# A hybrid encoder layer on one Trainium2 core: attention products one step later, the exponential ahead of the high part on ScalarE, and four smaller moves

## The chip, the cores and the metric

The kernel runs on one core of one Trainium2 chip, written in Bass with every engine's instruction stream and semaphores laid out by hand. The metric is device time in microseconds (us), the median of several executions; lower is better. Engines are named as in the profile: PE is TensorE (PEld its weight loads), DVE is VectorE, ACT is ScalarE, POOL is GpSimd, SP is SyncE, which issues most DMAs.

## The reference, cut to what matters

One encoder layer over 512 tokens of 1024 features: a long-convolution mixer and a grouped-query attention side by side, then attention over 256 memory rows, then a mixture of 16 experts. The change touches the attention and the two stages behind it:

```python
def attend_block(qblk):
    s = jnp.einsum('bkgqd,bksd->bkgqs', qblk, kt).astype(jnp.float32) * scale
    p = jax.nn.softmax(s, axis=-1).astype(vt.dtype)
    return jnp.einsum('bkgqs,bksd->bkgqd', p, vt)
...
y = jnp.concatenate([group_rms_norm(y_hy, out_norm_hyena[i], HYENA_GROUPS),
                     group_rms_norm(y_at, out_norm_attn[i], N_Q_HEADS)], axis=-1)
x = x + y @ w_out[i]
x = x + memory_cross_attn(rms_norm(x, norm_xattn[i]), rms_norm(mem, norm_mem[i]), ...)
x = x + hier_moe(rms_norm(x, norm_moe[i]), ...)
```

There are 8 query heads of 64 features over 2 key/value heads, and in the memory attention 4 heads of 128, whose keys are normalised per head by a root mean square and a gain.

## The kernel before, in words

Products that need more than one pass of precision are made from a high part (the value rounded to fp32r, by ScalarE) and a low part (value less high part, by VectorE), as three products: high by high, high by low, low by high. Weights come from HBM in pieces of 512 KB through a ring of three buffers: ScalarE makes `w_hi` of a piece (`weight_hi`, L744), VectorE `w_lo` (`weight_lo`, L1173), TensorE multiplies (`chunk_jobs`, L1987). Pieces 26 to 29 are the first half of the output projection (`wo0`), 30 to 33 the second (`wo1`), 34 to 37 the memory queries (`wq`).

**The attention loop** has 32 steps, one for 128 queries of one head. Step s, engine by engine:

- TensorE (`for s in range(-2, NSEQ)`): `score(s + 4)`, two products into a PSUM bank; `pt(s + 2)`, four transposes of the exponentials; at listed steps a transpose of further queries or keys (`QT_STEPS`, `KT_STEPS`), of the last head's output (`out_T`, `OT_STEPS`), the sums of squares of the convolution's output (`HN_STEPS`) or the transposes of its inverse norms (`hyena_inverse_T`, `HR_STEPS`); and at odd steps `pv(s // 2)`, the eight products with the values for steps s-1 and s.
- ScalarE: `gqa_pt_hi(s)`, the high part of the transposed exponentials (L911), then `gqa_exp(s + 2)` (L903), then at listed steps copies out of PSUM (`out_copy` L918, `out_rows` L924, `qT_evac` L880, `kT_evac` L876), squares (L884), a weight piece's high part, and once the square root of the convolution's sums (`hyena_root`, L889), which needs another activation table.
- VectorE: `gqa_max(s + 3)` (a reduction L1499 and a tiny product L1500), then `gqa_lo(s)`, the low part (L1506), then at listed steps a weight piece's low part, `out_sums` (L1512) and `hyena_norm` (L1477, L1484, L1485).
- GpSimd: `out_square` (L604), for the two memory row blocks `mk_normed` (L596, L597), and one copy that widens the 32 inverse norms of the convolution to `inv_wide` (L612).

A transposed pair of steps sits in one of two buffers, so `gqa_pt_hi(s)` waits until `pv(s // 2 - 2)` is done. Scores and transposes turn through six PSUM banks. `psum_jobs` is the one list by which every engine counts banks, so each table of steps is used there too.

**Behind the loop** TensorE transposes the normalised attention output (`yT_job`, four of them), finishes `wo0` (piece 29 needs all four), runs `wo1`, transposes the memory keys (`mkT`, which wait for `mk_normed`), then x, and multiplies `wq`. ScalarE makes the four high parts `yT_hi` (L749) and after them the pieces from 29 on. Then comes the memory attention: eight steps of score, exponential, normalisation by VectorE and transposes (L1932), and the products with the memory values (`mo`, L1925). The router and the experts follow; their instructions are not touched.

`constant_products(job, n)` (L1963) multiplies the identity by itself n times into a bank that will be overwritten; it computes nothing that is used.

Of the kernel before, what the change touches and what calls it, by code (L numbers as in the profile page):

```python
# [57 lines left out]

HR_STEPS = [17, 20, 24, 28]
GATED_STEP = 1  # L60
HN_STEPS = [8, 12]
MK_STEP = 9
QT_STEPS = [1, 5, 9, 11, 13, 15]
KT_STEPS = [3, 7]
EARLY = NQ - 2
EARLY_STEP = TT * EARLY + 5
OT_STEPS = [TT * h + 6 for h in range(NQ - 1)]
FILL = [3, 3, 2, 2] + [1] * 6


def psum_jobs():
# [21 lines left out]
    for s in range(-2, n):  # L93
        if s >= 0 and s % TT == 1:
            jobs += [("O", s // TT)]
        if s + 2 + AHEAD < n:
            jobs += [("S", s + 2 + AHEAD)]
        if s + 2 < n:
            jobs += [("PT", s + 2)]
        if s in OT_STEPS:  # L100
            jobs += [("OT", OT_STEPS.index(s))]
        if s in KT_STEPS:
            jobs += [("kT", 2 + KT_STEPS.index(s))]
        if s in QT_STEPS:
            jobs += [("qT", 2 + QT_STEPS.index(s))]
        if s in HN_STEPS:
            jobs += [("hn", HN_STEPS.index(s))]
        if s in HR_STEPS:
            jobs += [("hr", HR_STEPS.index(s))]
# [21 lines left out]
def build(nc, a, out, xn_dram, y_dram):  # L131
    with ExitStack() as ctx:
# [235 lines left out]
        s_pair = sem("ident_pair_ready")  # L368
        s_minv = sem("mk_inverse_ready")
        s_store = sem("xn_stored")  # L370
# [207 lines left out]
        def _(pool):  # L578
# [12 lines left out]
            pool.tensor_tensor(ident_pair[:], ident[:, 0:HD], ident[:, HD:P], ALU.add).then_inc(s_pair, 1)  # L591
            def mk_normed(j):

                pool.wait_ge(s_minv, 1)
                x3 = mk[:, j, :].rearrange("p (h d) -> p h d", d=MHD)
                link(pool.tensor_tensor(x3, x3, small[:, 40 + MH * j:44 + MH * j].unsqueeze(2).to_broadcast([P, MH, MHD]), ALU.mult))  # L596
                pool.tensor_tensor(x3, x3, row("gmk").unsqueeze(1).to_broadcast([P, MH, MHD]), ALU.mult).then_inc(s_mkn, 1)  # L597

            def out_square(h):

                wait_freed(pool, ("OT", h))
                if h >= 2:
                    pool.wait_ge(s_oss, h - 1)
                pool.tensor_tensor(o_sq[:, h % 2], out_head(h), out_head(h), ALU.mult).then_inc(s_osq, 1)  # L604

            out_square(0)
            mk_normed(0)
            out_square(1)
            mk_normed(1)
            out_square(2)  # L610
            pool.wait_ge(s_hrec, 1)
            pool.tensor_copy(inv_wide[:].rearrange("p t c w d -> p (t c w) d"),  # L612
                             small[:, 280:312].unsqueeze(2).to_broadcast([P, 8 * TT, HD])).then_inc(s_hwide, 1)

            for h in range(3, NQ):
                out_square(h)
# [68 lines left out]
        def _(act):  # L685
# [200 lines left out]
            def hyena_root():  # L886
                for n in range(len(HN_STEPS)):
                    wait_freed(act, ("hn", n))
                act.activation(small[:, 280:312], small[:, 280:312], ACT.Sqrt, bias=eps, scale=1.0 / HD).then_inc(s_hroot, 1)  # L889

            kT_evac(0)
            kT_evac(1)
# [41 lines left out]
            for s in range(NSEQ):  # L934
                gqa_pt_hi(s)
                if s + AHEAD < NSEQ:
                    gqa_exp(s + AHEAD)
                if s % TT == 0 and s > 0:
                    out_copy(s // TT - 1)
# [8 lines left out]
                if s == HN_STEPS[-1] + 1:  # L948
                    hyena_root()
                if s in (8, 10, 19):  # L950
                    weight_hi(26 + (8, 10, 19).index(s), 1)
                if s == EARLY_STEP:
                    act.activation(small[:, 398:399], eps, ACT.Sqrt)
                    out_root(0, EARLY, 4)
            out_copy(NQ - 1)
            out_rows(NQ - 1)
            out_root(EARLY, NQ, 5)
            for k in range(CT):
                split_hi(("yT", k), yT_hi[:, CT + k, :], col("attn_norm", k))
            weight_hi(29, 6)  # L960

# [181 lines left out]
        def _(dve):  # L1143
# [392 lines left out]
            for s in range(AHEAD + 1):  # L1536
                gqa_max(s)
            dve.wait_ge(s_hrms, 1)
            dve.reciprocal(small[:, 40:48], small[:, 40:48]).then_inc(s_minv, 1)
            dve.wait_ge(s_vhi, 1)  # L1540
# [35 lines left out]
            dve.wait_ge(ld["x2"], 16 * TT)  # L1576
            for k in range(CT):
                split_lo(("yT", k), yT_lo[:, CT + k, :], yT_hi[:, CT + k, :], col("attn_norm", k))
            weight_lo(29, 3)
            residual("wout", 0)  # L1580
            weight_lo(32, 4)
            residual("wout", 1)
# [335 lines left out]
        def _(pe):  # L1918
# [211 lines left out]
            def hyena_inverse_T(c):  # L2130

                if c == 0:
                    pe.wait_ge(s_hwide, 1)
                transposes(("hr", c), [inv_wide[:, t, c].rearrange("p w d -> p (w d)") for t in range(TT)])
# [65 lines left out]
            for s in range(-2, NSEQ):  # L2200
# [14 lines left out]
                for m in range(2 * (s - NSEQ) + 6, 2 * (s - NSEQ) + 8):  # L2215
                    if m >= 0:
                        output_tile(wo0 + m // TT, m % TT)
                if s >= 0 and s % 2 == 1:
                    pv(s // 2)
            output_tile(wo0 + 1, 2)  # L2220
# [38 lines left out]
            for s in range(MSEQ):  # L2259
                if s + MAHEAD < MSEQ:  # L2260
                    mem_score(s + MAHEAD)
                pe.wait_ge(s_mnorm, s + 1)
                transposes(("MPT", s), [pr[:, s % NPR, k * P:(k + 1) * P] for k in range(4)])
            for s in range(MSEQ):
                wait_freed(pe, ("MPT", s))
# [287 lines left out]
```

## Time and profile before

| what | us |
|---|---|
| median of 3 runs | 800.45 (798.2 to 801.01) |
| the profiled execution | 800.26 |
| its span (first to last instruction) | 798.4 |
| PE busy in the span | 748.8 |
| DVE busy | 605.4 |
| ACT busy | 460.1 |
| POOL busy | 86.2 |

The span is what the trace covers; the execution's own time is 1.86 us longer. Times in rows are us from the span's start. A matmul's row lasts from its start to the modelled end, so matmuls in a row overlap; the pitch is read from start to start. The same holds for ScalarE and VectorE, whose next instruction may start some 0.1 us before the last one's end. The attention loop lies at 258 to 346 us, the output projection to 387, the memory attention to 444, the router to 500, the experts to the end.

### The profile page before, as it was taken

To read this page: it belongs to the slowest core of one execution; us is meant where nothing else is said; L and a number is where in the kernel's file an instruction comes from. 1 tells how busy PE (TensorE), PEld (TensorE's weight loads), DVE (VectorE), ACT (ScalarE), POOL (GpSimd) and SP (SyncE) were. 2 spreads that over 40 slices of the span, in tenths; PEclk is the share of its full clock that TensorE was granted. 3 is DMA by queue.
4 is the path that set the end of the run, shared out by engine and by line. 5 is a ranking of instruction groups with operands and counts; after the bars stand their busy time and mean duration, and the time that the engine had idled before them with its cause. 6 is when DMAs were issued, how large, how long until landed. Compare 5 with 4: busy or idle time off the path is not lost.

```text
span 798.4 us, 10807 instructions
## 1 busy us (share of the span) xinstructions
PE 748.8 (94%) x3644; PEld 605.1 (76%) x3644; DVE 605.4 (76%) x926; ACT 460.1 (58%) x685; POOL 86.2 (11%) x99
## 2 busy tenths in 40 slices
PE   5899999999999888979897999999999999999994
PEld 3665858788898876768784787888888888888883
DVE  5767483996799879833547468899989989999882
ACT  5942333221243887531558332788788888887772
POOL 0000000000000022000000001123223233222111
PEclk9999999999999999999998997999999999999997
DMA  8730303020130200022130665999999999999841
GB/s 291 293 106 1 89 17 106 28 79 1 53 88 20 106 1 2 1 79 80 53 106 27 218 263 219 385 380 371 376 371 382 382 385 376 369 368 381 308 163 20
DMA packets 28542, 146.53 MB, mean 184 GB/s; under 512 B 4791, under 2 KB 6711, under 8 KB 21976
## 3 DMA queue, kind: packets, MB, share of 16 engines
q1 hardware_dynamic: 23320, 135.53, 45.5%
q0 software_dynamic: 5184, 10.50, 5.0%
q8 instruction: 23, 0.38, 0.2%
q14 instruction: 15, 0.12, 0.0%
HBM read 141.81 MB, written 12.58 MB: 193 GB/s over the span
## 4 chain that ended last, share of the span: by engine, by line
PE 70%; DVE 16%; ACT 6%; DMA 4%; issue 3%; SPq 0%; POOL 0%; DVEq 0%; ACTq 0%; POOLq 0%
PE bank L1987 17%; PE bank L2372 10%; PE bank L2374 10%; PE bank L2373 10%; PE bank L1925 10%; PE bank L1932 2%; DMA slot<-in_w_down 2%; PE bank L2367 2%; PE bank L1999 1%; DVE w_lo L1173 1%; DVE small L1499 1%; ACT w_hi L744 1%; ACT pr L1003 1%; PE bank L2286 1%; PE bank L2284 1%
## 5 line engine op out<-in xcount | busy, mean ns | idle before, releaser
L1844 DVE TENSOR_TENSOR e_lo<-slot,e_hi 128x1024 fp32r<-128x1024 f32 x192 | 221.5, 1219 | 9.8 <-ACT e_hi L1053 9.7
L1053 ACT ACTIVATE e_hi<-slot 128x1024 fp32r<-128x1024 f32 x192 | 188.2, 1060 | 8.5 <-DMA slot<-in_w_down 5.8
L1173 DVE TENSOR_TENSOR w_lo<-w_raw,w_hi 128x1024 fp32r<-128x1024 f32 x41 | 50.1, 1239 | 71.8 <-ACT w_hi L744 71.7
L744 ACT ACTIVATE w_hi<-w_raw 128x1024 fp32r<-128x1024 f32 x41 | 42.6, 1057 | 100.4 <-DMA w_raw<-in_w_in 63.4
L2372 PE MATMUL bank<-e_hi,hgT_hi 128*128 128x512 f32 x240 | 95.0, 396 | 0.3 <-DVE hgT_lo L1856 0.3
L2374 PE MATMUL bank<-e_hi,hgT_lo 128*128 128x512 f32 x240 | 93.6, 390 | 0.0
L2373 PE MATMUL bank<-e_lo,hgT_hi 128*128 128x512 f32 x240 | 93.4, 389 | 0.0
L2372 PEld LDWEIGHTS bank<-e_hi,hgT_hi 128*128 128x128 f32 x240 | 45.2, 189 | 9.5 <-DVE hgT_lo L1856 0.7
L2374 PEld LDWEIGHTS bank<-e_hi,hgT_lo 128*128 128x128 f32 x240 | 45.0, 188 | 9.6
L2373 PEld LDWEIGHTS bank<-e_lo,hgT_hi 128*128 128x128 f32 x240 | 45.1, 188 | 8.9
L2372 PE MATMUL bank<-e_hi,gaT_hi 128*128 128x512 f32 x120 | 48.1, 400 | 0.0
L2374 PE MATMUL bank<-e_hi,gaT_lo 128*128 128x512 f32 x120 | 46.9, 391 | 0.0
L2373 PE MATMUL bank<-e_lo,gaT_hi 128*128 128x512 f32 x120 | 46.8, 390 | 0.0
L1987 PE MATMUL bank<-hT_hi,w_hi 128*128 128x512 f32 x96 | 37.9, 395 | 0.0
L1987 PE MATMUL bank<-hT_lo,w_hi 128*128 128x512 f32 x96 | 37.4, 389 | 0.0
L1987 PE MATMUL bank<-hT_hi,w_lo 128*128 128x512 f32 x96 | 37.4, 389 | 0.0
L1987 PE MATMUL bank<-w_hi,hT_hi 128*128 128x512 f32 (+1 forms) x96 | 34.0, 354 | 0.8 <-DVE hT_lo L1179 0.8
L1987 PE MATMUL bank<-w_hi,hT_lo 128*128 128x512 f32 (+1 forms) x96 | 34.0, 354 | 0.0
L1987 PE MATMUL bank<-w_lo,hT_hi 128*128 128x512 f32 (+1 forms) x96 | 34.0, 354 | 0.0
L1932 PE MATMUL bank<-ident,pr 128*128 128x128 f32 x160 | 24.8, 278 | 9.6 <-ACT pr L903 5.3
L653 POOL DMA_INDIRECT out_dram<-eo,meta_i x16 | 25.5, 1595 | 74.5 <-ACT eo L1088 44.3
L1071 ACT ACTIVATE hgT_hi<-bank 128x512 fp32r<-128x512 f32 x28 | 15.2, 595 | 30.5 <-PE bank L2367 30.5
(395 smaller groups left out, 1674.5 us busy)
## 6 DMA issues: line engine op xcount, KB each, us to landing
slot<-in_w_down SPq DMA_DIRECT2D x16, 2048.0 KB, 17.1
slot<-in_w_gate SPq DMA_DIRECT2D x16, 2048.0 KB, 14.9
slot<-in_w_up SPq DMA_DIRECT2D x16, 2048.0 KB, 15.6
w_raw<-in_w_in SPq DMA_DIRECT2D x18, 512.0 KB, 3.6
w_raw<-in_w_out SPq DMA_DIRECT2D x8, 512.0 KB, 3.7
w_raw<-in_w_k_mem SPq DMA_DIRECT2D x4, 512.0 KB, 6.2
x_in<-in_x SPq DMA_DIRECT2D x4, 512.0 KB, 9.3
w_raw<-in_w_v_mem SPq DMA_DIRECT2D x4, 512.0 KB, 6.1
```

The source lines that it names most:

```text
L653: pool.indirect_dma_start(out[0], bass.IndirectOffsetOnAxis(ap=meta_i[:, q, 0:1], axis=0), eo[q][:], None, bounds_check=T - 1, oob_is_err= ...
L744: act.activation(w_hi[ring(m)][:], w_raw[ring(m)][:], ACT.Copy).then_inc(s_wh, 1)
L1053: act.activation(e_hi[buffer(b, j)][:], slot[slot_][:, 1024 * part:1024 * (part + 1)], ACT.Copy).then_inc(s_ehi, 1)
L1173: dve.tensor_tensor(w_lo[slot_][:], w_raw[slot_][:], w_hi[slot_][:].bitcast(F32), ALU.subtract)\
L1844: dve.tensor_tensor(e_lo[slot_][:, at_], slot[slot_][:, at_], e_hi[buffer(b, j)][:].bitcast(F32), ALU.subtract)\
L1925: ins = pe.matmul(dst, l, r, start=(n == 0), stop=(n == len(pairs) - 1))
L1932: ins = pe.transpose(bank(job)[:, n * width:(n + 1) * width], s, ident[:])
L1987: ins = pe.matmul(bank(job)[:, 0:width], left, right, start=(k == 0 and m == 0), stop=(final and m == 2))
L2367: ins = pe.transpose(banks[half][:, k * P:(k + 1) * P], hg[q][:, c:D:KT], ident[:])
L2372: pe.matmul(dst, act_hi, w_hi_, start=first, stop=False)
L2373: pe.matmul(dst, act_hi, w_lo_, start=False, stop=False)
L2374: return pe.matmul(dst, act_lo, w_hi_, start=False, stop=last)
```

## The change

1. `pv` of a pair runs one step later on TensorE: at even steps, with the last pair after the loop. The tables of steps shift to suit.
2. ScalarE runs `gqa_exp(s + 2)` before `gqa_pt_hi(s)`; `out_copy` comes one step later.
3. Weight: the high and low part of piece 29 are made before the fourth `yT` split, not after it.
4. Inverse: `inv_wide` is written by ScalarE in four parts, one for each use, not by GpSimd in one copy.
5. Keys: the memory keys are normalised by VectorE in the output projection, not by GpSimd in the attention loop.
6. Constants: constant products are added before each transpose job of the memory attention (6, then 1 each) and before its value products (5).

```diff
-HR_STEPS = [17, 20, 24, 28]
+HR_STEPS = [17, 21, 25, 29]
-HN_STEPS = [8, 12]
+HN_STEPS = [9, 13]
-QT_STEPS = [1, 5, 9, 11, 13, 15]
-KT_STEPS = [3, 7]
+QT_STEPS = [1, 5, 8, 10, 12, 14]
+KT_STEPS = [3, 6]
-EARLY_STEP = TT * EARLY + 5
-OT_STEPS = [TT * h + 6 for h in range(NQ - 1)]
+EARLY_STEP = TT * EARLY + 6
+OT_STEPS = [TT * h + 7 for h in range(NQ - 1)]
...
-            out_square(0)
-            mk_normed(0)
-            out_square(1)
-            mk_normed(1)
-            out_square(2)
-            pool.wait_ge(s_hrec, 1)
-            pool.tensor_copy(inv_wide[:].rearrange("p t c w d -> p (t c w) d"),
-                             small[:, 280:312].unsqueeze(2).to_broadcast([P, 8 * TT, HD])).then_inc(s_hwide, 1)
-            for h in range(3, NQ):
+            for h in range(NQ):
                 out_square(h)
...
+            def inverse_wide(c):
+                act.wait_ge(s_hrec, 1)
+                act.activation(inv_wide[:, :, c], small[:, 280:312].rearrange("p (t c w) -> p t c w", t=TT, c=CT)[:, :, c, :]
+                               .unsqueeze(3).to_broadcast([P, TT, 2, HD]), ACT.Copy).then_inc(s_hwide, 1)
...
             for s in range(NSEQ):
-                gqa_pt_hi(s)
                 if s + AHEAD < NSEQ:
                     gqa_exp(s + AHEAD)
-                if s % TT == 0 and s > 0:
+                gqa_pt_hi(s)
+                if s % TT == 1 and s > 1:
                     out_copy(s // TT - 1)
...
+                if s + 1 in HR_STEPS:
+                    inverse_wide(HR_STEPS.index(s + 1))
...
             for k in range(CT):
+                if k == CT - 1:
+                    weight_hi(29, 1)
                 split_hi(("yT", k), yT_hi[:, CT + k, :], col("attn_norm", k))
-            weight_hi(29, 6)
+            weight_hi(30, 5)
...
             for k in range(CT):
+                if k == CT - 1:
+                    weight_lo(29, 1)
                 split_lo(("yT", k), yT_lo[:, CT + k, :], yT_hi[:, CT + k, :], col("attn_norm", k))
-            weight_lo(29, 3)
+            weight_lo(30, 2)
             residual("wout", 0)
-            weight_lo(32, 4)
+            dve.wait_ge(s_hrms, 1)
+            link(dve.reciprocal(small[:, 40:48], small[:, 40:48]))
+            weight_lo(32, 1)
+            mk_normed(0)
+            weight_lo(33, 1)
+            mk_normed(1)
+            weight_lo(34, 2)
             residual("wout", 1)
...
-                if c == 0:
-                    pe.wait_ge(s_hwide, 1)
+                pe.wait_ge(s_hwide, c + 1)
...
-                if s >= 0 and s % 2 == 1:
-                    pv(s // 2)
+                if s > 0 and s % 2 == 0:
+                    pv(s // 2 - 1)
+            pv(2 * NQ - 1)
...
                 if s + MAHEAD < MSEQ:
                     mem_score(s + MAHEAD)
+                constant_products(("MPT", s), 6 if s == 0 else 1)
                 pe.wait_ge(s_mnorm, s + 1)
                 transposes(("MPT", s), [pr[:, s % NPR, k * P:(k + 1) * P] for k in range(4)])
+            constant_products(("mo", 0), 5)
```

The first place is ScalarE at steps 2 to 5 of the attention loop. The name `pr` is the exponential, `pT_hi` the high part, `oT` the copy of a head's output. Before:

```order
L911 ACTIVATE pT_hi<-bank 128x4x128
L903 ACTIVATE pr,small<-bank,small 128x512
L880 ACTIVATE qT<-bank 128x512
L884 ACTIVATE y_sq<-u 128x512
L911 ACTIVATE pT_hi<-bank 128x4x128
L903 ACTIVATE pr,small<-bank,small 128x512
L884 ACTIVATE y_sq<-u 128x512
L911 ACTIVATE pT_hi<-bank 128x4x128
L903 ACTIVATE pr,small<-bank,small 128x512
L918 ACTIVATE oT<-bank 128x512
```

And now:

```order
L891 ACTIVATE pr,small<-bank,small 128x512
L899 ACTIVATE pT_hi<-bank 128x4x128
L867 ACTIVATE y_sq<-u 128x512
L891 ACTIVATE pr,small<-bank,small 128x512
L899 ACTIVATE pT_hi<-bank 128x4x128
L859 ACTIVATE kT<-bank 128x512
L867 ACTIVATE y_sq<-u 128x512
L891 ACTIVATE pr,small<-bank,small 128x512
L899 ACTIVATE pT_hi<-bank 128x4x128
L906 ACTIVATE oT<-bank 128x512
```

Within a step the exponential now stands ahead of the high part, and the copy `oT` stands behind the next step's pair of them.

The second place is ScalarE behind the loop, at the four high parts of `yT`. Before:

```order
L930 ACTIVATE small<-small 128x4x2
L749 ACTIVATE yT_hi<-bank,cols 128x512 x4
L744 ACTIVATE w_hi_59<-w_raw_51 128x1024
L744 ACTIVATE w_hi_57<-w_raw_49 128x1024
L744 ACTIVATE w_hi_58<-w_raw_50 128x1024
```

And now:

```order
L918 ACTIVATE small<-small 128x4x2
L732 ACTIVATE yT_hi<-bank,cols 128x512 x3
L727 ACTIVATE w_hi_59<-w_raw_51 128x1024
L732 ACTIVATE yT_hi<-bank,cols 128x512
L727 ACTIVATE w_hi_57<-w_raw_49 128x1024
L727 ACTIVATE w_hi_58<-w_raw_50 128x1024
```

The first piece (29, in buffer 51) moved ahead of the fourth high part; VectorE's `w_lo` moved in the same way.

The third place is TensorE in the memory attention, from the first scores on. Before:

```order
L1932 MATMUL bank<-ident,mq 128x128 x16
L2253 MATMUL bank<-mkT,mqT 128x256 x8
L1932 MATMUL bank<-ident,pr 128x128 x4
L2253 MATMUL bank<-mkT,mqT 128x256 x2
L1932 MATMUL bank<-ident,pr 128x128 x4
```

And now:

```order
L1938 MATMUL bank<-ident,mq 128x128 x16
L2259 MATMUL bank<-mkT,mqT 128x256 x8
L1969 MATMUL bank<-ident 128x128 x6
L1938 MATMUL bank<-ident,pr 128x128 x4
L2259 MATMUL bank<-mkT,mqT 128x256 x2
L1969 MATMUL bank<-ident 128x128
L1938 MATMUL bank<-ident,pr 128x128 x4
```

Constant products (L1969) now stand in front of every transpose job; nothing else moved there.

## Rows read from the trace of the kernel before

**Rows 1.** Stretch, length, busy us (count) of PE, PEld, DVE, ACT, POOL; PEclk, DMA, GB/s

```profile
259.38:330.75 71.37, 60.73 (x449) 53.28 (x448) 60.95 (x119) 57.81 (x125) 10.44 (x11) 1.00 0.08 30
354.87:357.85 2.98, 0.00 (x1) 0.00 (x1) 2.03 (x3) 2.58 (x3) 0.00 (x0) 1.00 0.60 176
357.85:361.80 3.95, 3.95 (x10) 3.12 (x11) 2.90 (x3) 1.06 (x1) 0.00 (x0) 0.57 0.01 4
434.72:440.30 5.58, 5.58 (x7) 2.48 (x8) 4.19 (x4) 2.98 (x4) 0.00 (x0) 0.50 0.00 0
430.00:434.70 4.70, 1.98 (x13) 1.27 (x13) 2.35 (x10) 4.13 (x11) 0.00 (x0) 0.87 0.00 0
```

**Rows 2.** Waits, 259 to 331 us: total us, times, longest

```profile
ACT oT L918 <- PE bank L1925: 5.5, 7, 1.1
PE bank L1932 <- ACT pr L903: 5.3, 5, 2.5
PE bank L1925 <- DVE pT_lo L1506: 3.5, 4, 1.7
```

**Rows 3.** Timeline of PE, one wait early in the loop (start, length, [idle before])

```profile
273.36 0.49 PE L1963 MATMUL bank<-ident 128*128 128x128 f32 x2 [1.34 <-ACT pr L903]
```

**Rows 4.** Timeline of ACT and PE around the square root

```profile
293.54 1.28 ACT L889 ACT_TABLE_LOAD   x1 [1.40 <-DVE small L1493]
297.96 0.63 PE L1932 MATMUL bank<-ident,pr 128*128 128x128 f32 x4 [2.46 <-ACT pr L903]
```

**Rows 5.** GpSimd's copy, VectorE's tiny product beside it, and that product's usual length

```profile
300.49 1.90 POOL L612 COPY inv_wide<-small 128x2048 f32<-128x2048 f32 x1
300.72 1.68 DVE L1500 TENSOR_TENSOR small<-small 128x1 f32<-128x1 f32 x1
L1500 DVE TENSOR_TENSOR small<-small x32: 159/160/1680, 259.2 to 328.2; 128x1 f32<-128x1 f32 x32
```

**Rows 6.** Timeline of DVE: one step and the work on the convolution's output

```profile
304.31 0.41 DVE L1512 TENSOR_REDUCE small<-o_sq 128x4 f32<-128x256 f32 x1
304.63 0.68 DVE L1499 TENSOR_REDUCE small<-bank 128x1 f32<-128x512 f32 x1
305.43 0.69 DVE L1506 TENSOR_TENSOR pT_lo<-bank,pT_hi 128x512 fp32r<-128x512 f32 x1
306.03 0.74 DVE L1477 SCALAR_TENSOR_TENSOR u<-u,cols,bank 128x512 f32<-128x512 f32 x1
...
307.88 0.69 DVE L1499 TENSOR_REDUCE small<-bank 128x1 f32<-128x512 f32 x1
```

**Rows 7.** Timeline of ACT: one step; and the squares of 128x512 from SBUF

```profile
302.79 0.60 ACT L911 ACTIVATE pT_hi<-bank 128x512 fp32r<-128x512 f32 x1
303.27 0.79 ACT L903 ACTIVATE pr<-bank,small 128x512 f32<-128x512 f32 x1
...
304.03 0.62 ACT L911 ACTIVATE pT_hi<-bank 128x512 fp32r<-128x512 f32 x1
...
L884 ACT ACTIVATE y_sq<-u x4: 618/634/646, 266.2 to 273.2; 128x512 f32<-128x512 f32 x4
```

**Rows 8.** The load of piece 29, and such loads' time to landing

```profile
338.87 0.38 SPq L494 DMA_DIRECT2D w_raw<-in_w_out  x1
...
w_raw<-in_w_out SPq DMA_DIRECT2D x8, 512.0 KB, 3.7
```

**Rows 9.** Timeline at piece 29: ACT, DVE, PE

```profile
354.90 0.69 ACT L749 ACTIVATE yT_hi<-bank,cols 128x512 fp32r<-128x512 f32 x1 [6.21 <-PE bank L1932]
355.62 0.75 DVE L1179 SCALAR_TENSOR_TENSOR yT_lo<-bank,cols,yT_hi 128x512 fp32r<-128x512 f32 x1 [5.72 <-ACT yT_hi L749]
357.85 0.50 PE L1987 MATMUL bank<-w_hi,yT_hi 128*128 128x512 f32 x1 [2.98 <-DVE w_lo L1173]
```

**Rows 10.** Timeline of PE: two products of 128x512 in `wo0`, before that

```profile
353.58 0.39 PE L1987 MATMUL bank<-w_hi,yT_hi 128*128 128x512 f32 x1
353.81 0.39 PE L1987 MATMUL bank<-w_lo,yT_hi 128*128 128x512 f32 x1
```

More of the change, by code:

```diff
@@ L93, in psum_jobs @@
     for s in range(-2, n):
-        if s >= 0 and s % TT == 1:
+        if s >= 0 and s % TT == 2:
             jobs += [("O", s // TT)]
@@ L368, in build @@
         s_pair = sem("ident_pair_ready")
-        s_minv = sem("mk_inverse_ready")
         s_store = sem("xn_stored")
@@ L591, in _ @@
             pool.tensor_tensor(ident_pair[:], ident[:, 0:HD], ident[:, HD:P], ALU.add).then_inc(s_pair, 1)
[L592 to L597, printed above, removed]
             def out_square(h):
@@ L954, in _ @@
                     out_root(0, EARLY, 4)
+            out_rows(NQ - 2)
             out_copy(NQ - 1)
@@ L1537, in _ @@
                 gqa_max(s)
-            dve.wait_ge(s_hrms, 1)
-            dve.reciprocal(small[:, 40:48], small[:, 40:48]).then_inc(s_minv, 1)
             dve.wait_ge(s_vhi, 1)
@@ L1577, in _, with mk_normed @@
             for k in range(CT):
+                if k == CT - 1:
+                    weight_lo(29, 1)
                 split_lo(("yT", k), yT_lo[:, CT + k, :], yT_hi[:, CT + k, :], col("attn_norm", k))
-            weight_lo(29, 3)
+            weight_lo(30, 2)
             residual("wout", 0)
-            weight_lo(32, 4)
+            def mk_normed(j):
+                x3 = mk[:, j, :].rearrange("p (h d) -> p h d", d=MHD)
+                link(dve.tensor_tensor(x3, x3, small[:, 40 + MH * j:44 + MH * j].unsqueeze(2).to_broadcast([P, MH, MHD]), ALU.mult))
+                dve.tensor_tensor(x3, x3, row("gmk").unsqueeze(1).to_broadcast([P, MH, MHD]), ALU.mult).then_inc(s_mkn, 1)
+            dve.wait_ge(s_hrms, 1)
[5 more added lines that the diff above has]
+            weight_lo(34, 2)
             residual("wout", 1)
```

## The prediction

> **What bounds the kernel now.** I read the stretches first (busy time and granted clock), then the waits of the attention loop, then the timelines of ACT, DVE and PE at the places that the change touches, and last the load of piece 29. TensorE is busy 748.8 of the 798.4 us, so time is to be had only where it waits or runs at the lower clock. [Rows 1] show four such places: the loop up to its last exponential, 71.37 us of which TensorE works 60.73, so 10.6 us is the most that the loop can give; 2.98 us without a product ahead of piece 29; the 3.95 us behind that at a granted clock of 0.57, which is near the lower of TensorE's two levels (1.2 against 2.4 GHz); and 5.58 us at 0.50 in the memory attention, with TensorE busy throughout. What is saved there should last to the end: from the memory attention on, the work hangs on TensorE's progress, and the experts keep it busy.
>
> In the loop no engine is full: DVE works 60.95 and ACT 57.81 of 71.37. The waits in [rows 2] are a ring: TensorE's transposes wait for exponentials (5.3 us), its value products for low parts (3.5 us), ScalarE's copy of a head's output for TensorE (5.5 us in 7).
>
> **The change, part by part, against the profiled execution's own 800.26** (the median of the runs is 800.45, so nothing has to be shifted).
>
> *Values one step later.* The copy `oT` no longer stands in ScalarE's queue waiting for products just issued: they are a step old. At the first place where this reaches TensorE the wait is 1.34 us [rows 3]; I take 1.3 off. The copy waited 5.5 us in all, but most of that lay beside TensorE's own work, so no more is taken. Nothing of TensorE's work is added; the last pair of products moves behind the loop, where only the last head's output waits for it.
>
> *The square root.* ScalarE's queue holds a table load of 1.28 us behind a wait of 1.40, and TensorE then waits 2.46 [rows 4]. With one exponential more issued ahead of the root, and VectorE's sums no longer behind a weight piece, I take the wait to be 1.8: 0.65 off. Ends: 0 (the table load stays as it is, and decides) and 1.4.
>
> *Inverse and keys off GpSimd.* Beside GpSimd's copy of 1.90 us VectorE's tiny product took 1.68 us, where its usual time is 0.16 [rows 5]. So VectorE's chain gets back 1.5 us. The Trainium skill says in "SBUF — State Buffer", section "Who interferes with whom", that VectorE and GpSimd share a pair of ports as an exclusive lock, which blocks a VectorE operation with two SBUF inputs beside a GpSimd one that reads SBUF; the trace agrees, with the 1.68 against 0.16. VectorE's 1.5 us is TensorE's too where the ring binds, and I take all of it; the lower end is 0 (TensorE waits for ScalarE's root there anyway). In return VectorE gets four multiplications and one reciprocal in the output projection. Each is no longer than its 0.74 us of 128x512 [rows 6], together 3.2 us; VectorE waits for TensorE in that stage (5.72 us at one place, below), which covers them, and without that cover they would cost up to 3.2. I take 0. ScalarE gets four parts, each of 128x512 elements as `y_sq` is: about 0.63 us each [rows 7], 0.52 where the next starts early, 2.1 us in all.
>
> *Exponential ahead of the high part.* This has a price. VectorE's step is 0.80 us for the maximum and its product, 0.60 for the low part; a sum of squares 0.32, a step of the convolution's norm 1.85 (306.03 to 307.88) [rows 6]. ScalarE's is 0.76 for the exponential, 0.48 for the high part, whose result is there after 0.60 [rows 7]. Count from VectorE's maximum for step 22, at 0: it is there at 0.80, exp(22) ends at 1.58, high part 20 is there at 2.18, and VectorE comes to low part 20 at 2.20: no stall. Now ScalarE does a copy and an inverse part (0.8), exp(23) ends at 3.6, high part 21 is there at 4.19 against 3.61 wanted: 0.6 lost. The copy `oT` (0.49) in the next step gives 5.91 against 5.6: 0.3 lost. The norm's 1.85 then lets ScalarE catch up. So 0.9 per group of four steps where inverse parts are made, three groups, 2.7 us. Against it stand TensorE's waits for low parts, 3.5 us in 4 [rows 2], which exponentials issued sooner should shorten; I set 1.5 against it and book 1.2 as cost. Ends: −2.3 (all 3.5 go, and the ring costs only 1.2) and +2.7 (none goes). The Trainium skill says in "TensorE: Matmul & The Clock Gate", section "Architectural detail: the array is 16× 32×32, not 1× 128×128", that ScalarE's and VectorE's queues keep strict order. That speaks against this edit: a ready high part stays behind an exponential whose maximum is late. Read by itself, it would turn the 1.2 into the full 2.7.
>
> *The last inverse* stands between exponentials of steps 30 and 31 now; the transposes of the fourth block come later by its 0.5. I book 0.5.
>
> **Loop:** −1.3 −0.65 −1.5 +1.2 +0.5 = −1.8 us (rounded).
>
> *Weight.* Piece 29 is issued at 338.87 and such a load lands after 3.7 us [rows 8], so at 342.6. ScalarE is idle 6.21 us before the fourth `yT_hi` at 354.90, VectorE 5.72 before `yT_lo` at 355.62 [rows 9]; w_hi and w_lo (at most 0.95 and 1.3 us, by what is left of the second stretch of [rows 1] beside those rows) fit in. TensorE then waits for `yT_lo` alone, ready at 355.62 + 0.75 = 356.37, and starts at 356.45 instead of 357.85: 1.4 off. Three of the 24 products of that piece don't need `yT_lo` of the fourth and run in the wait, at a pitch of 0.23 [rows 10]: 0.7 off. The ends are 1.0 and 2.8.
>
> *Clock behind piece 29.* The stretch at 0.57 holds 10 products in 3.95 us [rows 1]; at 0.23 they take 2.3: 1.6 off, if the clock stays up. Before it TensorE had 2.98 us without a product; now it would have about 1.2. In the loop it waits 2.46 [rows 4] while the granted clock of the loop stays at 1.00 [rows 1]. So I expect it to stay. Ends: 0 and 1.6.
>
> *Constants.* 18 constant products of 128x128, two of which take 0.49 us [rows 3]: 4.4 us at most. Before the low stretch TensorE works 1.98 of 4.70 us while ScalarE works 4.13 [rows 1]; the 6 and the first ones fill 2.7 of idle there, and the last 5 stand where the value products wait for ScalarE's high parts. So they cost about 0, and at most 4.4 − 2.7 = 1.7. If they hold the clock, 5.58 us at 0.50 become 2.79: 2.8 off. If they don't: 0.
>
> **Sum:** 1.8 + 2.1 + 1.6 + 2.8 = 8.3; 800.26 − 8.3 = 792.0 us.
>
> **The rivals.** About 0.5% (4 us) is what a measurement of this kernel can tell from no change.
>
> 1. *The ring is looser than worked out.* ScalarE has 13 us free in the loop, and all waits for low parts go: the loop gives 1.8 + 1.2 + 3.5 = 6.5, the time is 787.3. Against it: the same engines carry 2 us more.
>
> 2. *The clock doesn't do what the edits want.* The constants are few, and single ones between steps may not hold it: 5.5 gained, 794.8. If only the stretch behind piece 29 stays low, 6.7 gained, 793.6. Both low: 1.8 + 2.1 = 3.9, 796.4. For it: the clock fell after a stretch in which TensorE worked 1.98 of 4.70, and gaps between the single constants remain. This is also the case in which that part of the change doesn't do what it says.
>
> 3. *The order on ScalarE binds in every head.* The 0.9 us are lost in seven groups of four steps instead of three, 6.3, and nothing is set against them: the loop is −1.3 −0.65 −1.5 +6.3 +0.5 = +3.3, the time 800.26 + 3.3 − 6.5 = 797.1.
>
> 4. *Slower: ScalarE and VectorE take turns throughout.* With the exponential ahead, the chain maximum, exponential, high part, low part goes round once a step, and whatever else ScalarE does in a step adds to VectorE's time. VectorE by pitches: 30 × 1.40 + 4 × 1.85 + 7 × 0.32 + 3 × 1.3 = 55.5. ScalarE's other work: 57.81 − 30 × 1.24 = 20.6, with the inverse parts 22.7. Sum 78.2 against 71.37: +6.8, +0.5 for the last inverse, −2.1 at piece 29, and with TensorE waiting this often no gain by the clock: 805.5. It decides from where ScalarE's other work in a step passes what VectorE has beside maximum and low part. Against it: the norms' 1.85 and the weight pieces on VectorE stand in just those steps, and hide ScalarE's.
>
> **How the numbers follow.** Forecast 0.50; rival 1, 0.12; rival 2, 0.18 (0.12 for one place, 0.06 for both); rival 3, 0.12; rival 4, 0.08. The ends of the terms move the forecast's own time by some 4 us both ways, which rival 1 and rival 3 lie at. The range is 786.0 to 798.5: it takes in the first four cases but for the tails of the forecast's bounds, and leaves out rival 4. Faster by over 0.5% (below 796.3): 0.12 + 0.12 + the forecast's 0.50 less a tail of 0.05 + half of the 0.06: 0.72. Within 0.5%: the rest of those and rival 3, 0.20. Slower: 0.08.
>
> **What would show it.** In the loop's stretch TensorE's idle time falls from 10.6 to about 9; the 1.34 is gone and the longest tiny product is near 0.16; VectorE's waits for `pT_hi` grow, by the 2.7. If these grow by 6 and the loop is longer than 71.4 us, rival 3 or 4 is right; if they vanish, rival 1. Ahead of piece 29 the gap is 1.2 or less, and no stretch behind it is below 0.9 of the clock. In the memory attention the stretch at 0.50 is gone: if it is there and full of constants, rival 2. My prediction is wrong if the loop is longer than before, or if the gains are there and the experts end no sooner.

## The result, and the profile after

The changed kernel takes 795.09 us (median of 8 runs, 792.18 to 797.21) against 800.16 for the kernel before beside it: a ratio of 0.9933, 95% interval 0.9915 to 0.9950. That is 5.1 us less, where 8.3 were forecast; it lies inside the forecast range, and the interval ends at the 0.5% that the prediction took as what can be told from no change. The execution that was profiled took 792.18 us, the fastest of the eight, so its trace shows more gain (8.1 us) than the median.

Stretches of the changed kernel's span: length, busy us (count) of PE, PEld, DVE, ACT, POOL, then granted clock, DMA share, GB/s. They stand beside [rows 1], the last but one beside the last row there.

```profile
259.23:328.72 69.49, 60.70 (x442) 53.31 (x442) 57.04 (x116) 58.03 (x128) 3.69 (x6) 0.99 0.09 31
354.92:355.78 0.86, 0.00 (x1) 0.01 (x1) 0.75 (x1) 0.86 (x2) 0.00 (x0) 1.00 0.72 198
355.78:359.18 3.40, 3.40 (x15) 2.83 (x16) 1.77 (x2) 1.16 (x2) 0.00 (x0) 1.00 0.26 99
425.58:430.28 4.70, 3.79 (x29) 3.08 (x28) 2.55 (x11) 4.08 (x11) 0.00 (x0) 1.00 0.00 0
430.28:437.40 7.12, 7.12 (x18) 3.29 (x18) 5.38 (x6) 4.06 (x6) 0.00 (x0) 1.00 0.00 0
```

Ahead of piece 29 TensorE is without work for 0.86 us instead of 2.98, and the clock stays at 1.00 behind it. In the memory attention TensorE is busy 3.79 instead of 1.98 of the 4.70 us, and the clock stays up there too.

The loop's first row looks better than it is. The exponentials now run earlier in ScalarE's order, so the last one (328.72) is no longer the same landmark. From the transposes of the keys ahead of the loop to the first transposes of `yT` behind it, the same work on TensorE in both kernels, the loop is only 0.5 us shorter. First the kernel before, then the changed one, in the same columns:

```profile
254.81:346.02 91.21, 80.11 (x562) 69.98 (x561) 72.20 (x140) 65.62 (x140) 12.10 (x14) 1.00 0.09 30
```

```profile
254.65:345.35 90.70, 81.51 (x562) 71.44 (x561) 68.78 (x139) 66.91 (x144) 5.24 (x9) 0.98 0.09 30
```

The 0.98 is a stretch at the lower clock level that the loop before did not have in its profiled execution: 3.4 us at 0.50, with TensorE busy throughout, so 1.7 us lost. It follows the loop's last wait for an exponential.

```profile
326.74 1.12 PE L1938 MATMUL bank<-ident,pr 128*128 128x128 f32 x4 [1.74 <-ACT pr L891]
```

```profile
326.80:330.20 3.40, 3.40 (x17) 3.40 (x17) 1.72 (x4) 3.01 (x8) 0.62 (x1) 0.50 0.03 5
```

The waits of the changed kernel from 259 to 331 us (total, times, longest) answer to [rows 2]:

```profile
DVE pT_lo L1499 <- ACT pT_hi L899: 11.3, 14, 3.3
ACT pr L891 <- DVE small L1493: 8.4, 6, 3.6
PE bank L1938 <- ACT pr L891: 7.4, 8, 1.8
...
PE bank L1938 <- DVE pT_lo L1499: 0.5, 2, 0.3
ACT oT L906 <- PE bank L1931: 1.3, 2, 0.9
```

TensorE's waits for low parts went from 3.5 to 0.5 us and ScalarE's copy waits from 5.5 to 1.3. In return TensorE waits 7.4 us for exponentials (5.3 before), and ScalarE and VectorE wait for each other 19.7 us. Which part of the change did the one and which the other is what the runs were for.

### The profile page after: what moved, and what is told of

Read it like the earlier page. It is cut to its first block, busy times and chain, and to the rows that moved or that the text cites. A ratio compares the mean times of both kernels' runs of the same rounds, so it can differ in the third digit from the quotient of the medians.

```text
span 790.3 us, 10886 instructions
## 1 busy us (share of the span) xinstructions
PE 746.5 (94%) x3680; PEld 606.8 (77%) x3680; DVE 604.0 (76%) x930; ACT 461.1 (58%) x689; POOL 76.3 (10%) x94
## 4 chain that ended last, share of the span: by engine, by line
PE 68%; DVE 14%; ACT 7%; DMA 5%; issue 3%; SPq 1%; POOL 0%; ACTq 0%; POOLq 0%; DVEq 0%
PE bank L1993 16%; PE bank L2380 10%; PE bank L2382 10%; PE bank L2381 10%; PE bank L1931 9%; PE bank L1938 3%; DMA slot<-in_w_down 2%; PE bank L2375 2%; PE bank L2005 1%; DMA x_in<-in_x 1%; ACT pr L891 1%; PE bank L2294 1%; PE bank L2292 1%; PE bank L2293 1%; PE bank L2417 1%
```

## The experiments

Each ratio is to the kernel before on the same chip, with its 95% interval, from 5 to 12 executions of each kernel. "Loop" is the length between the two landmarks in the run's one profiled execution; "low" is the time in it at the lower clock level, and each such stretch of about 3.4 us costs about 1.7 where TensorE is busy throughout.

| run | median us | ratio | loop us | low in it |
|---|---|---|---|---|
| kernel before | 800.16 | 1 | 91.21 | none |
| changed kernel | 795.09 | 0.9933 (0.9915 to 0.9950) | 90.70 | one stretch |
| after_again | 795.27 | 0.9931 (0.9912 to 0.9951) | 90.26 | one |
| hi_first | 790.42 | 0.9878 (0.9859 to 0.9896) | 86.35 | none |
| only_values | 795.79 | 0.9951 (0.9934 to 0.9967) | 87.76 | one |
| only_weight | 796.90 | 0.9952 (0.9933 to 0.9971) | 91.20 | none |
| only_constants | 799.32 | 0.9979 (0.9963 to 0.9996) | 93.33 | two |
| hi_inverse_gpsimd | 791.57 | 0.9888 (0.9870 to 0.9906) | 86.85 | none |
| hi_keys_gpsimd | 791.15 | 0.9875 (0.9857 to 0.9894) | 87.96 | one |
| hi_no_constants | 791.48 | 0.9884 (0.9864 to 0.9905) | 87.94 | one |
| inverse_gpsimd | 794.12 | 0.9934 (0.9911 to 0.9956) | 88.68 | none |
| ahead_first_half | 791.94 | 0.9898 (0.9871 to 0.9925) | 86.86 | none |
| ahead_second_half | 795.06 | 0.9937 (0.9916 to 0.9958) | 91.22 | two |
| max_ahead | 806.85 | 1.0078 (1.0052 to 1.0104) | 104.37 | three, one of 7 us |

### after_again: the changed kernel once more

> The changed kernel once more, for a second look at where its time goes in another execution. Theory A (the clock varies from execution to execution): about 795 us, 0.993 of before; its place-by-place gains are those of the first trace (the first of the last yT transposes 0.5 us earlier than before relative to the loop's start, piece 29 another 1.4, the value products of the memory attention no longer at 0.50 of the clock), and what it is slower than 792.18 us lies in one or more further stretches of 3 to 7 us at 0.5 of the clock while TensorE is busy. Theory B (the queues vary): the same time, but no further low stretch; TensorE's waits in the loop are longer by 2 us or more than the 8.7 us of the first trace.

The execution took 793.89 us. The places agree with the first trace within 0.1 us (piece 29 starts at 355.74, the memory value products at 430.30), and TensorE's waits for exponentials are 7.3 against 7.4 us. TensorE's waits do not vary (VectorE's for high parts are 10.5 against 11.3). The loop's low stretch is there again, but at another place: from 318.2 on, at the end of a wait of 1.27 us, a wait that the first trace had as well (1.26 us at 317.87) with no fall behind it.

```profile
318.24 1.11 PE L1938 MATMUL bank<-ident,pr 128*128 128x128 f32 x4 [1.27 <-ACT pr L891]
```

```profile
317.87 0.66 PE L1938 MATMUL bank<-ident,pr 128*128 128x128 f32 x4 [1.26 <-ACT pr L891]
```

The first of these rows is from this run, the second from the changed kernel's first trace; the four transposes take 1.11 us at the low clock and 0.66 at the full one. Of the 1.7 us between the two profiled executions (793.89 against 792.18) 1.0 has come up by the end of the router: the experts' first product starts at 493.99 against 493.00. The clock is low there from 485.4 to 492.2 here, and in the first trace in two pieces of half that length (470.1 to 473.5 and 487.2 to 490.6). The other 0.7 lies behind, among the experts, where this trace has one more low stretch (775.5 to 778.9). So theory A holds: the waits are the same, and the low stretches are what differs. How much each of them costs is not worked out.

### hi_first: the exponential behind the high part again

```diff
             for s in range(NSEQ):
+                gqa_pt_hi(s)
                 if s + AHEAD < NSEQ:
                     gqa_exp(s + AHEAD)
-                gqa_pt_hi(s)
```

> The changed kernel with the high part ahead of the exponential on ScalarE again, and nothing else undone. By the prediction's term (exponential ahead costs 1.2 us, between -2.3 and +2.7): faster than the changed kernel by 1.2, about 793.9 us, and VectorE's waits for pT_hi in the loop fall from 11.3 to below 8 us. Rival (the exponential ahead is what makes the loop shorter): slower than the changed kernel by 1 to 3 us, 796 to 798, with TensorE's waits for exponentials above 7.4 us or for low parts above 0.5.

The direction was right, the size was not: 790.42 us, 4.9 under the changed kernel in the same comparison by the medians and 4.2 by the ratios, with intervals that do not meet (0.9859 to 0.9896 against 0.9912 to 0.9951). The exponential ahead costs about 4 us, not 1.2; from the two intervals I estimate 2 to 6.4. A second pair of runs below differs in nothing but this order, with the inverse norms on GpSimd in both: hi_inverse_gpsimd and inverse_gpsimd are 3.7 us apart by the ratios (0.9888 against 0.9934; an estimate of 1.4 to 6.0). The loop is 86.35 us against 90.26 and 90.70. Of the 4.35 to the first trace, 1.7 is the low stretch and 2.65 are waits; against after_again it is 2.2 of waits, and in the second pair, where neither loop has a low stretch, 1.8 (86.85 against 88.68). Waits of hi_first from 259 to 331 us:

```profile
DVE pT_lo L1499 <- ACT pT_hi L899: 5.0, 8, 1.5
...
PE bank L1938 <- ACT pr L891: 5.6, 8, 1.9
...
ACT pr L891 <- DVE small L1493: 3.2, 4, 1.9
```

VectorE and ScalarE now wait 8.2 us for each other, not 19.7. This kernel beats both kernels of the case.

### ahead_first_half and ahead_second_half: where the cost lies

```diff
-                if s + AHEAD < NSEQ:
+                if s < NSEQ // 2:
                     gqa_exp(s + AHEAD)
                 gqa_pt_hi(s)
+                if not (s < NSEQ // 2) and s + AHEAD < NSEQ:
+                    gqa_exp(s + AHEAD)
```

(the other run has the two halves exchanged).

> The changed kernel with the exponential ahead of the high part in steps 0 to 15 only, behind it from step 16 on. If the cost of 4.9 us lies at the square root (step 14) and in the squares and copies of the first half: about the changed kernel's 795. If it lies in the steps with norms and inverse parts (16 on), with the low clock they bring: about hi_first's 790.5.

> The counterpart: exponential ahead in steps 16 to 29 only. Cost in the second half: about 795, with TensorE's waits for exponentials of 1.7 us and a low stretch of the clock behind step 20; cost in the first: about 790.5. If both runs lie at 792 to 793.5, it is spread over the whole loop.

The first: 791.94 us, loop 86.86. The second: 795.06, loop 91.22 with two low stretches. So most of the cost lies in steps 16 on, where the convolution's norms stand on VectorE: 4.7 us by the ratios. In its trace, the low stretches left out, the loop of ahead_second_half is some 1.5 us longer than hi_first's, and one of its two low stretches begins at 300.0, right behind the square root, where the order is still hi_first's. In steps 0 to 15 the order costs about 1.6 us by the ratios (0.9898 against 0.9878, intervals overlap) and nothing by the traces up to the square root: the transposes that end the square root's gap start 42.73 us behind the loop's first landmark in the changed kernel (297.38) and 42.70 in hi_first (298.66).

In the second half the two traces can be laid beside each other by ScalarE's four inverse parts, one per group of steps. First the changed kernel, then hi_first:

```profile
299.59 0.66 ACT L876 ACTIVATE inv_wide<-small 128x512 f32<-128x512 f32 x1
...
308.47 0.64 ACT L876 ACTIVATE inv_wide<-small 128x512 f32<-128x512 f32 x1
...
318.46 0.64 ACT L876 ACTIVATE inv_wide<-small 128x512 f32<-128x512 f32 x1
...
327.33 0.63 ACT L876 ACTIVATE inv_wide<-small 128x512 f32<-128x512 f32 x1
```

```profile
300.45 0.62 ACT L876 ACTIVATE inv_wide<-small 128x512 f32<-128x512 f32 x1
...
308.09 0.62 ACT L876 ACTIVATE inv_wide<-small 128x512 f32<-128x512 f32 x1
...
316.97 0.62 ACT L876 ACTIVATE inv_wide<-small 128x512 f32<-128x512 f32 x1
...
324.74 0.63 ACT L876 ACTIVATE inv_wide<-small 128x512 f32<-128x512 f32 x1
```

The groups take 8.88, 9.99 and 8.87 us against 7.64, 8.88 and 7.77: 1.1 to 1.2 more in each of three, 3.45 together. Behind the last of them the changed kernel gives some back, so that the whole loop without its low stretch is only 2.65 longer. What happens in one is seen on DVE and ACT of the changed kernel:

```profile
310.39 0.69 DVE L1499 TENSOR_TENSOR pT_lo<-bank,pT_hi 128x512 fp32r<-128x512 f32 x1 [0.56 <-ACT pT_hi L899]
...
312.12 0.69 DVE L1499 TENSOR_TENSOR pT_lo<-bank,pT_hi 128x512 fp32r<-128x512 f32 x1 [0.25 <-ACT pT_hi L899]
...
315.43 0.70 DVE L1478 TENSOR_TENSOR yT_lo<-u,yT_hi 128x512 fp32r<-128x512 f32 x1
316.04 0.68 DVE L1492 TENSOR_REDUCE small<-bank 128x1 f32<-128x512 f32 x1
316.76 0.16 DVE L1493 TENSOR_TENSOR small<-small 128x1 f32<-128x1 f32 x1
```

```profile
316.95 0.78 ACT L891 ACTIVATE pr<-bank,small 128x512 f32<-128x512 f32 x1 [3.61 <-DVE small L1493]
317.63 0.19 ACT L891 ACTIVATION_READ_ACCUMULATOR pr<-bank,small 128x1 f32 x1
317.72 0.59 ACT L899 ACTIVATE pT_hi<-bank 128x512 fp32r<-128x512 f32 x1
```

The exponential stands 3.61 us in ScalarE's queue for a maximum that VectorE has behind a norm, and the high part stands behind it until 317.72. Earlier in the same group VectorE loses 0.56 and 0.25 us waiting for high parts, and what VectorE loses the next maximum is later: 0.81 of the 1.1. In hi_first ScalarE makes the high part first and only the exponential waits:

```profile
313.45 0.60 ACT L899 ACTIVATE pT_hi<-bank 128x512 fp32r<-128x512 f32 x1 [0.51 <-PE bank L1931]
315.94 0.78 ACT L891 ACTIVATE pr<-bank,small 128x512 f32<-128x512 f32 x1 [1.89 <-DVE small L1493]
```

Queues in strict order are what the Trainium skill states for ScalarE and VectorE ("TensorE: Matmul & The Clock Gate", section "Architectural detail: the array is 16× 32×32, not 1× 128×128"). The rows agree: the high part at 317.72 starts only when the exponential of 316.95 is through.

### inverse_gpsimd: is it the inverse parts on ScalarE?

```diff
-            for h in range(NQ):
+            for h in range(3):
+                out_square(h)
+            pool.wait_ge(s_hrec, 1)
+            pool.tensor_copy(inv_wide[:].rearrange("p t c w d -> p (t c w) d"),
+                             small[:, 280:312].unsqueeze(2).to_broadcast([P, 8 * TT, HD])).then_inc(s_hwide, 1)
+            for h in range(3, NQ):
                 out_square(h)
...
-                if s + 1 in HR_STEPS:
-                    inverse_wide(HR_STEPS.index(s + 1))
...
-                pe.wait_ge(s_hwide, c + 1)
+                if c == 0:
+                    pe.wait_ge(s_hwide, 1)
```

> The changed kernel (exponential ahead) with the inverse norms widened by GpSimd in one copy again. The exponential ahead has cost 4.9 us with ScalarE's four inverse parts in the loop. Theory A (the prediction's ring: inverse parts on ScalarE make the high part late, 0.9 us in each of three groups of steps): the cost shrinks without them, 2 us or more faster than the changed kernel, 793 or less, and VectorE's waits for pT_hi fall from 11.3 to below 8. Theory B (every exponential in front delays the high part, inverse parts or not): within 1.5 us of the changed kernel, 794 to 797.

794.12 us, ratio 0.9934 against the changed kernel's 0.9933 and 0.9931: theory B. VectorE's waits for high parts fall to 8.3 us, less than theory A asked, and the loop, 88.68 without a low stretch, is what the changed kernel's is without its own (90.70 − 1.7 = 89.0). So ScalarE's extra 2.1 us do not make the cost. What is left in these steps is VectorE's own work, the norms and a weight piece's low part; no run takes that away, so that it decides is read from the rows above and not shown by an edit.

### max_ahead: the maximum one step earlier

```diff
-            for s in range(AHEAD + 1):
+            for s in range(AHEAD + 2):
                 gqa_max(s)
...
-                if s + AHEAD + 1 < NSEQ:
-                    gqa_max(s + AHEAD + 1)
+                if s + AHEAD + 2 < NSEQ:
+                    gqa_max(s + AHEAD + 2)
```

> The changed kernel with VectorE's maxima one step further ahead (the maximum of step s+4 in its step s, not of s+3), the exponential still ahead of the high part. Theory A (the high part is late because the exponential in front of it waits for a maximum that stands behind a norm or a sum on VectorE): ScalarE's waits for maxima in the loop fall from 8.4 to below 4 us, the low stretch in the loop is gone, and the time is 3 to 5 us under the changed kernel's, 790 to 792. Theory B (the high part is late by the 0.76 us of every exponential ahead of it, whatever the maximum does): within 1.5 us of the changed kernel, 794 to 796.5, with VectorE's waits for pT_hi still above 9 us.

Both theories missed: 806.85 us, slower than before, with a loop of 104.37. The maximum now stands in VectorE's queue ahead of its score, and VectorE waits 23.4 us for TensorE, while ScalarE's waits for maxima are down to 0.6:

```profile
DVE small L1492 <- PE bank L1931: 23.4, 18, 3.8
```

The low parts queued behind it come late for TensorE in turn (8.9 us at the transposes). The run therefore does not test theory A: it took the late maximum away and put a worse wait in its place. That the cost goes when the maximum is never late stays unshown; shown is that it is in the half with the norms and goes when the high part stands in front.

### only_values: the products one step later, alone

The edit is part 1 of the change, with the copy `oT` one step later, which the list names under part 2: the tables of steps, `pv(s // 2 - 1)` at even steps and the last pair behind the loop, the last copies of rows in their new order.

> The kernel before with the products with the values one step later (and the tables, the copy and the square root's place that go with it) alone; the high part ahead of the exponential as before. By the prediction's terms: -1.3 for the early wait and -0.65 for the root, +0 elsewhere, 798.2 to 798.6 against 800.2. Rival (this edit is what made hi_first's loop 3.7 us shorter, and keys and inverse hardly count): 3 to 4 us less, 796 to 797.5, with TensorE's waits for low parts in the loop gone from 3.5 to below 0.5.

795.79 us, 0.9951: the rival is right, 3.9 us instead of 1.95. The waits of TensorE in the loop are

```profile
PE bank L1937 <- ACT pr L906: 5.3, 5, 1.9
PE bank L1968 <- ACT pr L906: 0.4, 1, 0.4
```

and none is for a low part any more. The 3.5 us in 4 of [rows 2] are gone by this edit alone; products that start a step later find the low parts ready. The early wait is 0.4 us, down from 1.34 [rows 3]. Its loop is 87.76 with a low stretch in it, some 86.1 without: 5 us shorter than before, and as short as hi_first's, so the moves off GpSimd add nothing to the loop. That the time falls by less than 5 fits the low stretches, but the interval of the 3.9 (2.6 to 5.3) takes in the 5 as well.

### only_weight and only_constants

> The kernel before with piece 29's high and low part ahead of the fourth yT split alone. By the prediction: 2.1 us by the shorter wait and 1.6 by the clock, 3.7 in all (796.5 us), TensorE's wait at piece 29 falls from 2.98 to about 0.9 us and no low stretch follows. Rival (the low stretch is only moved): 2.1 us less, 798.1, and a stretch of 3 to 4 us at 0.5 within the output projection all the same.

> The kernel before with the constant products of the memory attention alone. By the prediction: 2.8 us less than before (797.4 against 800.2), and the value products of the memory attention start at the same place but take 7.1 us instead of 9.9, with the granted clock at 1.00. Rival (the clock merely falls at another place soon after, or the constants push the chain back): within 1 us of before, with a low stretch in the next 30 us that the kernel before does not have.

only_weight: 0.9952, 3.8 us, as forecast (3.7). In its trace TensorE waits 0.86 us at piece 29, which starts 10.43 us behind the first `yT` transposes against 11.83 in the kernel before; from there to the transposes of the memory queries it takes 55.49 us against 57.94. So 1.4 at the wait and 2.45 behind it, where 0.7 + 1.6 were booked. The rival (the low stretch only moves) can be counted over all traces: right behind piece 29 the clock is low in each of the three without this edit (the kernel before, only_values, only_constants) and in none of the eleven with it. In two of the eleven, hi_no_constants and ahead_first_half, it falls some 34 us later, at 387, in hi_no_constants at the third of three waits in 5 us, for x, the memory keys and x's low part (0.40, 0.89 and 0.80 us), and costs 1.7 there. So the edit does what it says, and what it saves is now and then lost again further on.

only_constants: 0.9979, 1.7 us, between the two theories; the interval (0.3 to 3.0 us) does not decide between them. No low stretch follows in the next 30 us, so the rival's sign is missing. Its own memory attention does what was expected, 7.11 us for the value products at 1.00; the clock stays up there in all ten traces with the constants. But the fall that they prevent is not there every time without them. Without constants the products start behind about the same wait, 1.10 us at 434.72 before (9.88 us in all) and 1.09 us here, in only_weight:

```profile
430.83 7.11 PE L1929 MATMUL bank<-mpT,mv 128*128 128x512 f32 x16 [1.09 <-ACT mpT L1015]
```

Of four traces without constants two are low there (the kernel before and hi_no_constants, 9.72 us) and two are not (only_weight, only_values). In the two that are, the wait of 1.10 us is not what the fall followed: the clock is at 0.50 from 433.5 in the kernel before, when that wait begins, and from 428.9 in hi_no_constants, 0.4 us ahead of it. What stands before both falls are the transposes with their gaps (1.98 us of work in 4.70, [rows 1]). Half of 2.7 is 1.4 us, which is what both comparisons find within their intervals.

### Parts undone from hi_first

hi_keys_gpsimd puts `mk_normed` back on GpSimd behind the first two squares; hi_inverse_gpsimd has the diff of inverse_gpsimd; hi_no_constants drops both calls of `constant_products` in the memory attention.

> hi_first with the inverse norms widened by GpSimd in one copy again, ahead of the fourth square. Theory A (the prediction's contention term): slower than hi_first by 1.5 us, about 792, with one of VectorE's tiny products or pairs of SBUF operands at 1.5 us or more beside the copy, and TensorE waiting there. Theory B (ScalarE's four parts cost as much as VectorE gets back, 2.1 against 1.5): within 1 us of hi_first, 789.5 to 791.5.

> hi_first with the memory keys normalised by GpSimd behind the first two squares again. The prediction gave this move 0. Theory A: within 1 us of hi_first, 789.5 to 791.5. Theory B (VectorE's products of two SBUF operands stand beside GpSimd's at 278 and 288 us and the loop pays for it): slower by 1 to 2.5 us, 791.5 to 793, with tiny products (usual 0.16 us) of 0.8 us or more and a weight piece's low part of 1.9 in place of 1.2.

> hi_first without the constant products in the memory attention. By the prediction: slower by 2.8 us, 793.2, with the memory value products at 0.5 of the clock in every execution. Theory B (whether the clock falls there varies from execution to execution, as only_weight kept it without constants): slower by 0.5 to 2 us, 791 to 792.5.

hi_inverse_gpsimd: 0.9888 against 0.9878, 0.8 us with overlapping intervals, and a loop 0.5 us longer. The collision is there as in [rows 5], on another product of the same kind:

```profile
301.27 1.68 DVE L1496 TENSOR_TENSOR small<-small 128x1 f32<-128x1 f32 x1
```

So VectorE does lose 1.5 us there, and the loop, without a low stretch in either trace, loses 0.5, as theory B has it (what VectorE gets back ScalarE spends). By the times theory A's 1.5 us is not excluded. hi_keys_gpsimd: 0.9875 against 0.9878, no difference, though two tiny products of 0.85 us are back. hi_no_constants: 0.9884 against 0.9878, 0.5 us, nearer to theory B; its own trace has the fall. None of the three is told from hi_first by its interval.

## Why the prediction was right, and where it was off

The time lies in the range and the sign is right. That it is only 3.2 us off the forecast is in part luck: the products one step later gave 2 us more than booked, the exponential ahead lost 3 more, and the inverse norms and the constants gave about 1 less each.

- **Values one step later, and the root:** booked −1.95, measured alone −3.9 (only_values; 0.9934 to 0.9967, that is −5.3 to −2.6). The early wait and the root went nearly as worked out (0.4 us is left of 1.34 in only_values, none in the changed kernel; the root's 2.46 is 1.85 in only_values and 1.75 in the changed kernel, 1.8 was taken). What was missed is that this edit also removes TensorE's waits for low parts, 3.5 us.
- **Exponential ahead:** booked +1.2, measured +4.2 (hi_first against after_again, estimated 2 to 6.4) and +3.7 (the pair with the inverse norms on GpSimd). This is the step that failed. The hand-worked ring was right in kind and near in size: it gave stalls of 0.6 and 0.3 us in each of three groups, the trace has 0.56 and 0.25 and groups 1.1 to 1.2 us longer. For the whole loop without low stretches the traces have 1.8 to 2.65 us, where 2.7 was worked out. The error is the "I set 1.5 against it": the waits for low parts that this credit came from were already gone by the other edit (none in only_values with the high part first, 0.5 us with the exponential ahead). The rest of the measured 4, some 1.5 to 2 us, is not placed, and by the intervals it need not be there. It is not simply the low stretch of the changed kernel's loop: with the exponential ahead throughout, two of three traces have one (not inverse_gpsimd), and with the high part first and the products one step later three of five (only_values, hi_keys_gpsimd, hi_no_constants). The reading by strict queues alone, the full 2.7, was the better one.
- **Inverse and keys off GpSimd:** booked −1.5, measured 0 (keys) and −0.8 (inverse, not told from 0, and from −1.5 neither); in the loops, −0.5. The tiny product is indeed back at 0.16 us everywhere. The lock on the shared ports that the Trainium skill describes ("SBUF — State Buffer", section "Who interferes with whom") is in the rows wherever the copy is on GpSimd: 1.68 us in hi_inverse_gpsimd, 1.46 in inverse_gpsimd, 1.24 in only_values, against 0.16. Most of it does not reach TensorE.
- **Last inverse:** booked +0.5; no run prices it by itself.
- **Weight:** 3.7 booked, 3.8 measured. The 1.4 at the wait is exact. The prediction expected the clock to stay up because it did so behind the wait of 2.46 us in the loop [rows 4]; that was no ground, for in only_constants, with the same instructions, the clock falls 1.6 us behind that wait (at 300.0).
- **Constants:** 2.8 booked, 1.7 measured on the kernel before and 0.5 on hi_first. The size of a fall was right (9.88 − 7.10 = 2.8), but the fall happens in two of four traces without the constants, not always.

Of the rivals, none happened as described. Rival 2's times (793.6 to 796.4) hold the result, but the clock stayed up at both of its places in the changed kernel. Rival 3 had the right place (the order on ScalarE) but in seven groups; the rows show it in three. By the check that the prediction gave for itself, VectorE's waits for `pT_hi` grew by 5.7 us, between its own 2.7 and the 6 that would have spoken for rival 3.

The parts measured alone add up: −3.9 (values) −3.8 (weight) −1.7 (constants) −0.8 (inverse) are −10.2 us, hi_first has −9.8 (0.9878 × 800 is 790.2), and with the exponential ahead +4.2 by the ratios the changed kernel's −5.4. Each part has an interval of 1.3 us or more on either side, so the agreement is no proof that the parts do not act on each other. The best version of these is hi_first: the whole change but for the order of exponential and high part.

## What to carry to other kernels

When two edits could both remove one wait, book the wait once, with the edit that reaches it first, and cost the other edit as if it were gone. An instruction whose input is ready should not be put behind one whose input may be late on a queue in strict order, even if the ring closes on paper in the plain step; look at the step in which the late engine does its extra work. And a wait removed from a side engine (here VectorE's collision with GpSimd) is worth only what the traced chain of the main engine shows at that place.

## What the runs showed of the hardware that was not expected

The granted clock falls at varying places. Loops with the same instructions had no low stretch in the kernel before and in only_weight, but two of about 3.4 us in only_constants, for a loop 2.1 us longer (93.33 against 91.20); those of after_again and the first trace had one each, 8 us apart. The wait of 1.26 us was followed by a fall in one execution and not in the other, and the gaps between the transposes of the memory attention in two traces of four. Where it falls in the loop seems to go with the order on ScalarE, though the counts are small: behind the square root in five of nine traces with the high part first in that half and in none of four with the exponential ahead (a wait of 1.85 or 2.46 us there against 1.75), and from step 16 on in one of nine with the high part first and in three of four with the exponential ahead. max_ahead, which has three, is left out of this count. So a low stretch in one profile is worth its length times half times how often it comes, and comparing single profiles misleads. The first pair of traces gave 8.1 us, the medians 5.1.
